# First norm applied at the evictions, x loaded in column blocks, and state space tables built from repeated rows

## What is computed

```python
h = rms_norm(x, norm_g)                      # x * rsqrt(mean(x*x) + eps) * g
g_q, g_k, ..., f_gate = split(h @ w_in)      # first layer: linear attention and forgetting attention
...
bb_re = coef_re[..., None] * br_ - coef_im[..., None] * bi_     # S5 layer: 128 groups of 16 channels,
bb_im = coef_re[..., None] * bi_ + coef_im[..., None] * br_     # 64 complex states each
```

## Time and profile before

| | |
|---|---|
| median of 3 runs | 3414.6 us (3409.22 to 3414.64) |
| profiled execution | 3409.54 us, span 3407.7 us |
| TensorE, VectorE, ScalarE, GpSimd busy | 98%, 48%, 38%, 15% |
| granted TensorE clock, mean | 0.994 |

### The profile page before, as it was taken

One profiled execution on the slowest core, in us unless ns is written; L12 is line 12 of the kernel. 1 busy time (PEld: TensorE's weight loads), 2 busy tenths in 40 slices (PEclk: granted clock), 3 DMA queues, 4 the chain that ended last, 5 costly groups with the idle time before them and its releaser, 6 DMA issues.

```text
span 3407.7 us, 41780 instructions
## 1 busy us (share of the span) xinstructions
PE 3330.7 (98%) x16431; PEld 2695.1 (79%) x16431; DVE 1635.8 (48%) x2695; ACT 1304.6 (38%) x2010; POOL 515.3 (15%) x749
## 2 busy tenths in 40 slices
PE   7999999999999999999999999999999999999998
PEld 6777887888888888888888776788878888777886
DVE  7895654344343444444344655553424343355433
ACT  4443433343233333433242646532323323355432
POOL 0001312322110000110330111121000111110211
PEclk8999999999999999999999999999999999999999
DMA  6776433546348777454335443363433643433642
GB/s 208 221 226 200 135 106 102 159 137 220 131 160 225 200 210 211 153 171 129 128 107 179 128 142 107 124 207 124 142 88 115 205 146 117 133 112 109 205 147 93
DMA packets 279523, 525.06 MB, mean 154 GB/s; under 512 B 64189, under 2 KB 99588, under 8 KB 274720
## 3 DMA queue, kind: packets, MB, share of 16 engines
q1 hardware_dynamic: 223504, 340.79, 33.2%
q0 software_dynamic: 53648, 178.32, 15.4%
q10 hardware_dynamic: 2176, 3.28, 0.4%
HBM read 408.32 MB, written 113.97 MB: 153 GB/s over the span
## 4 chain that ended last, share of the span: by engine, by line
PE 73%; ACT 3%; DVE 3%; issue 2%; DMA 1%; POOL 0%; ACTq 0%; POOLq 0%; DVEq 0%
PE pg L631 64%; PE pm L1322 2%; PE pm L1351 2%; PE pm L1338 1%; PE pm L2423 1%; ACT whi L390 1%; DMA mx_g<-zt 1%; PE pm L2427 0%; PE pm L2411 0%; DVE d_x L2511 0%; ACT stage L501 0%; ACT w_p L1387 0%; PE pm L2402 0%; PE pm L1816 0%; DVE wlo L396 0%
## 5 line engine op out<-in xcount | busy, mean ns | idle before, releaser
L396 DVE TENSOR_TENSOR wlo<-raw,whi 128x1024 fp32r<-128x1024 f32 x523 | 662.3, 1271 | 1237.1 <-ACT whi L390 1236.1
L390 ACT ACTIVATE whi<-raw 128x1024 fp32r<-128x1024 f32 x523 | 548.9, 1054 | 1093.6 <-PE pg L631 1084.0
L631 PE MATMUL pg<-a_hi,whi 128*128 128x512 f32 x1856 | 742.6, 400 | 11.2 <-DVE wlo L396 4.7
L631 PE MATMUL pg<-a_hi,wlo 128*128 128x512 f32 x1856 | 725.8, 391 | 0.0
L631 PE MATMUL pg<-a_lo,whi 128*128 128x512 f32 x1856 | 724.9, 391 | 0.0
L631 PE MATMUL pg<-b_hi,whi 128*128 128x512 f32 x1568 | 622.8, 397 | 7.4 <-DVE stage L572 3.2
L631 PE MATMUL pg<-b_hi,wlo 128*128 128x512 f32 x1568 | 612.2, 390 | 0.0
L631 PE MATMUL pg<-b_lo,whi 128*128 128x512 f32 x1568 | 611.7, 390 | 0.0
L631 PEld LDWEIGHTS pg<-a_hi,whi 128*128 128x128 f32 x1856 | 347.7, 187 | 90.2 <-issue 14.3
L631 PEld LDWEIGHTS pg<-a_hi,wlo 128*128 128x128 f32 x1856 | 347.2, 187 | 77.3
L631 PEld LDWEIGHTS pg<-a_lo,whi 128*128 128x128 f32 x1856 | 348.0, 187 | 73.3 <-issue 2.6
(11 more groups left out here) (442 smaller groups left out, 3846.1 us busy)
## 6 DMA issues: line engine op xcount, KB each, us to landing
raw<-in_l_w_in SPq DMA_DIRECT2D x169, 512.0 KB, 3.7
raw<-in_ab_w_in SPq DMA_DIRECT2D x112, 512.0 KB, 3.8
zt<-stage POOLq DMA_DIRECT2D x142, 256.0 KB, 3.5
raw<-in_c_w_in SPq DMA_DIRECT2D x64, 512.0 KB, 5.3
raw<-in_l_w_out SPq DMA_DIRECT2D x64, 512.0 KB, 4.0
raw<-in_ab_w_out SPq DMA_DIRECT2D x32, 512.0 KB, 4.0
raw<-in_glu_w SPq DMA_DIRECT2D x32, 512.0 KB, 4.1
raw<-in_c_w_out SPq DMA_DIRECT2D x32, 512.0 KB, 3.7
```

What stands on the lines that cost most here:

```text
L390: nc.scalar.activation(used(whi, n), used(raw, n), ACT.Copy).then_inc(hi_ready, 1)
L396: nc.vector.tensor_tensor(used(wlo, n), used(raw, n), used(whi, n).bitcast(F32), ALU.subtract).then_inc(lo_ready, 1)
L631: ins = nc.tensor.matmul(pg[m][:r.rows(m), :r.cols()], lhsT, rhs, start=(kt == 0 and n_pass == 0), stop=(kt == r.kts - 1 and n_pass == 2))
```

## The change

Two parts. **First norm at evictions.** `GLA_IN`, `FOX_IN` and `AB_GATES` join the scaled phases: the operand is x times the gain alone, and the evictions multiply by the deviation (transposed regions by VectorE at L572, the others by ScalarE). x is loaded in column blocks of 2, 2, 5 and 7 tiles; four tiles are turned before the first product and twelve within the first six half pieces after the first. ScalarE squares the token rows at half pieces 7 to 10, into `stage`. SyncE loads pieces 0 to 2 before the state space parameters and all other vectors. The first layer's attention uses a tile of its own instead of `rstd`. The preparation starts behind 7 pieces instead of 4.

**Tables by rows.** The powers are turned once (8 transposes) and stored; for each slice scaled B is turned (2 transposes) and stored as rows, and four loads of 512 KB (`repeat_rows`) bring both back repeated over 128 partitions, where VectorE multiplies them one slice later. `s_L` and its 16 transposes per slice are gone; `s_BT` is stored by its own semaphore.

```diff
-    SCALED = {n: C_U0 for n in (C_U0, C_REST)}
+    SCALED = {n: GLA_IN for n in (GLA_IN, FOX_IN, AB_GATES)}
+    SCALED.update({n: C_U0 for n in (C_U0, C_REST)})
...
+                r.deviation = 1 if SCALED[n] == GLA_IN else JOINTS[SCALED[n]]["devs"] + 1
...
+    X_BLOCKS = ((0, 2), (2, 4), (4, 9), (9, 16))
+    LAST_FRONT_UNIT = 6
+
     def turn_in_pool(pool):
+        for n, (k0, k1) in enumerate(X_BLOCKS):
+            if n == 2:
+                pool.wait_ge(raw_in[2], 16)
+            columns = slice(k0 * P, k1 * P)
+            pool.dma_start(XT["x_tok"][:, :, columns], inp["x"][0, :, columns].rearrange("(t p) d -> p t d", p=P)).then_inc(tokens_moved[n], 16)
+
+    def x_landed(eng, kt):
+
+        for n, (k0, k1) in enumerate(X_BLOCKS):
+            if k0 <= kt < k1:
+                eng.wait_ge(tokens_moved[n], 16)
+
+    def front_tiles(unit):
+
+        return range(2 * unit + 2, 2 * unit + 4) if 0 < unit <= LAST_FRONT_UNIT else ()
...
+        for kt in range(MT):
+            turn_x_pe(pe, kt)
+        pe.wait_ge(cols_ready, 1)
...
+    def first_block_pe(pe, unit):
+
+        for kt in front_tiles(unit):
+            turn_x_pe(pe, kt)
+        if unit == 10:
+            pe.wait_ge(s5_th, 1)
+            pe.wait_ge(xt_ev, 13)
+            for i in range(3):
+                ins = nc.tensor.transpose(pm[0][:, i * NPAIR:(i + 1) * NPAIR], s5_natural(i), ident[:NPAIR, :NPAIR])
+            ins.then_inc(s5_ct, 1)
+        if unit == 12:
+            pe.wait_ge(consts_in, 16 * NCONST)
+            pe.wait_ge(xt_ev, KT)
+            for r in range(2):
+                w = min(NROWS - r * P, P)
+                ins = nc.tensor.transpose(pm[1][:, r * P:r * P + w], rows[:w, r, :], ident[:w, :w])
+            ins.then_inc(cols_turned, 1)
+            pe.wait_ge(sd_ready, 1)
+            for t in range(NTOK):
+                ins = nc.tensor.matmul(pm[2][:, t * P:(t + 1) * P], rstd_col[:, t:t + 1].broadcast_to([P, P]), ident[:, :], start=True, stop=True)
+            ins.then_inc(rs_ready, 1)
...
+        split_hi(act, 0)
+        act.wait_ge(cols_ready, 1)
+        for kt in range(MT):
+            operand_hi(act, kt)
+        split_hi(act, 1)
+        split_hi(act, 2)
...
+    def first_block_act(act, unit):
+
+        for kt in front_tiles(unit):
+            operand_hi(act, kt)
+        if 7 <= unit < 7 + NTOK:
+            t = unit - 7
+            for c in range(NTOK):
+                act.wait_ge(tokens_moved[c], 16)
+            if t:
+                act.wait_ge(acc_done, KT // NTOK * t)
+            nc.scalar.activation(stage[:, :, :].rearrange("p m t -> p (m t)"), XT["x_tok"][:, t, :], ACT.Square,
+                                 accum_out=rstd_col[:, t:t + 1]).then_inc(acc_done, KT // NTOK)
+        if unit == 11:
+            s = lambda n: T5["s_small"][:, n, :]
+            act.wait_ge(acc_done, KT)
+            serial(act, act_seq)(nc.scalar.activation(rstd_col[:, :], rstd_col[:, :], ACT.Ln, scale=1.0 / D, bias=eps[:, 0:1]))
+            nc.scalar.activation(rstd_col[:, :], rstd_col[:, :], ACT.Exp, scale=-0.5).then_inc(sd_ready, 1)
...
+    def operand_lo(dve, kt):
+
+        dve.wait_ge(xt_ev, kt + 1)
+        dve.wait_ge(nh_ready, kt + 1)
+        nc.vector.scalar_tensor_tensor(out=A["a_lo"][:, kt, :], in0=XB["xb"][:, kt, :], scalar=col("ab_norm_g", kt),
+                                       in1=A["a_hi"][:, kt, :].bitcast(F32), op0=ALU.mult, op1=ALU.subtract).then_inc(h_ready, 1)
+
+    def tiles_dve(dve, tiles):
+
+        for n, kt in enumerate(tiles):
+            dve.wait_ge(xt_ready, kt + 1)
+            nc.vector.tensor_copy(XB["xb"][:, kt, :], pm[kt % 4][:, :]).then_inc(xt_ev, 1)
+            if n:
+                operand_lo(dve, kt - 1)
+        for kt in tiles[-1:]:
+            operand_lo(dve, kt)
 
     def turn_in_dve(dve):
+        dve.wait_ge(cols_turned, 1)
+        nc.vector.tensor_copy(cols[:, :KT], pg[3][:, :KT]).then_inc(cols_ready, 1)
+        dve.wait_ge(cols_ready, 1)
+        for kt in range(2):
+            dve.wait_ge(xt_ready, kt + 1)
+            nc.vector.tensor_copy(XB["xb"][:, kt, :], pm[kt][:, :]).then_inc(xt_ev, 1)
+        split_lo(dve, 0)
+        for kt in range(2):
+            operand_lo(dve, kt)
+        tiles_dve(dve, range(2, MT))
+        split_lo(dve, 1)
+        split_lo(dve, 2)
...
+        def repeat_rows(sl):
+
+            js = slice(sl * SPAIR, (sl + 1) * SPAIR)
+            over_rows = lambda name, n: V5[name][:, n, :, :].rearrange("p j x -> p (j x)")
+            for n in range(2):
+                power = powers_rows[n][:, js, :].rearrange("e j x -> e (j x)").unsqueeze(1)
+                sp.dma_start(over_rows("s_Pr", n), power.broadcast_to([ST, SC, SPAIR * P])).then_inc(rows_repeated, 16)
+                b = b_rows[sl][n].rearrange("(a c j) x -> a c (j x)", a=1, c=SC)
+                sp.dma_start(over_rows("s_Br", n), b.broadcast_to([ST, SC, SPAIR * P])).then_inc(rows_repeated, 16)
...
+            if at == 0 and sl == 0:
+                sp.wait_ge(s5_bte, 1)
+                sp.dma_start(powers_rows.rearrange("n (h e) j x -> (e j) (n h) x", e=2), V5["s_BT"][:, 0, :, :]).then_inc(rows_kept, 16)
+            if at == 3 and 0 < sl <= SSL:
+                sp.wait_ge(s5_l, 2 * sl)
+                sp.dma_start(bt_dram[sl - 1], V5["s_BT"][:, :, :, :].rearrange("p n j x -> p (n j x)")).then_inc(b_tables_kept, 16)
+            if at == 3 and 0 <= sl < SSL:
+                sp.wait_ge(s5_bte, sl + 2)
+                sp.dma_start(b_rows[sl].rearrange("n p x -> p n x"), V5["s_bT"][:, :, :]).then_inc(rows_kept, 16)
+            if at == 4 and 0 <= sl < SSL:
+                sp.wait_ge(rows_kept, 16 * (sl + 2))
+                repeat_rows(sl)
             if at == 5 and 0 <= sl < SSL:
-                sp.wait_ge(s5_bte, 2 * sl + 2)
-                keep(bt_dram, V5["s_BT"][:, :, :, :].rearrange("p n j x -> p (n j x)"), sl)
...
-        def turn_b(sl, n):
-            pe.wait_ge(s5_l, 2 * sl + n + 1)
-            if n == 0:
-                pe.wait_ge(s5_cc, sl + 1)
-            else:
-                pe.wait_ge(s5_ke, sl)
-            for j in range(SPAIR):
-                ins = nc.tensor.transpose(pm[2 * n + j // 4][:, j % 4 * P:(j % 4 + 1) * P], V5["s_L"][:, n, j, :, :], ident[:, :])
+        def turn_powers():
...
+        def turn_b(sl):
+            pe.wait_ge(s5_b, sl + 1)
+            pe.wait_ge(s5_bte, sl + 1)
+            for n in range(2):
+                ins = nc.tensor.transpose(pm[3][:, n * P:(n + 1) * P], V5["s_B"][:, n, :, :].rearrange("p c j -> p (c j)"), ident[:, :])
+            ins.then_inc(s5_bt, 1)
...
         def b_powers(sl, n):
-            js = slice(sl * SPAIR, (sl + 1) * SPAIR)
-            power = lambda c: ang[:, c, :ST, js].rearrange("p e j -> p j e").unsqueeze(3).broadcast_to([P, SPAIR, ST, SC])
-            b3 = lambda x: V5["s_B"][:, x, :, :].unsqueeze(2).broadcast_to([P, SPAIR, ST, SC])
             if n == 0:
-                dve.wait_ge(s5_b, sl + 1)
-                dve.wait_ge(s5_sc, 3)
-            else:
+                dve.wait_ge(rows_repeated, 16 * ROW_LOADS * (sl + 1))
+                dve.wait_ge(rows_kept, 16)
+                dve.wait_ge(b_tables_kept, 16 * sl)
+            to, by, tp = V5["s_BT"][:, n, :, :], V5["s_Pr"], t.rearrange("p j e c -> p j (e c)")
+            run(tt(to, V5["s_Br"][:, n, :, :], by[:, 0, :, :], ALU.mult))
+            run(tt(tp, V5["s_Br"][:, 1 - n, :, :], by[:, 1, :, :], ALU.mult))
+            tt(to, to, tp, ALU.subtract if n == 0 else ALU.add).then_inc(s5_l, 1)
+            if n == 0:
                 dve.wait_ge(s5_l, 2 * sl + 1)
...
-                if at in (1, 2):
-                    b_powers(sl, at - 1)
                 if at in (3, 4):
                     c_powers(sl, at - 3)
                 if at == 5:
                     phase(sl)
                 if at == 5 and sl == 0:
                     own_channel()
+            if at in (1, 2) and 0 < sl <= SSL:
+                b_powers(sl - 1, at - 1)
...
+        load_piece(sp, 0)
+        sp.wait_ge(made, 7)
+        vector("ab_norm_g", ident_in)
+        load_piece(sp, 1)
+        load_piece(sp, 2)
+        for n, name in enumerate(("s5_lambda_re", "s5_lambda_im")):
+            sp.dma_start(s5_natural(n), inp[name][0].rearrange("(j g) p -> j (g p)", g=2)).then_inc(s5_nat, 16)
+        sp.dma_start(T5["s_pw"][:NPAIR, 1, 0, :2], inp["s5_log_step"][0].rearrange("(j g) -> j g", g=2)).then_inc(s5_nat, 16)
+        sp.dma_start(T5["s_kv"][:, :], inp["steps"][:, :]).then_inc(s5_nat, 16)
+        load_piece(sp, 3)
...
-        beside(prep_sp(sp), PREP_STEPS, sp, sp_piece, GLA_IN, 4)
+        beside(prep_sp(sp), PREP_STEPS, sp, sp_piece, GLA_IN, 7)
```

238 lines of the change are left out of this document (104 added, 134 removed).

## The result

The changed kernel takes 3512.5 us (median of 4 runs, 3505.7 to 3516.0), the kernel before 3414.6 on the same chip: a ratio of 1.0284, 95% interval [1.0271, 1.0298]. It is 98 us slower; I had forecast 3418, with 3446 as the upper end. The profiled execution has a span of 3511.4 us, against 3407.7.

What follows compares the result with a forecast made beforehand. TensorE, 98% busy, was taken as the bound, VectorE right behind and binding in the new slices. The preparation stage summed to 306.7 against 304.5 us (+2.2), moved evictions +1.4: +3.6, giving 3418; range 3398 to 3446.

Steps and rivals of the forecast that it cites:

- The start: Kernel start: first product at 11.3 us (bounds 10 and 14), first 12 matmuls cold, no stall before 60.
- The lead steps and the slices without waits: State space preparation: lead steps 19.0 us, slices 1 to 7 bound by VectorE at 174.5 us before waits.
- Rows in time: Rival, slices: stored rows and loads land 4 us or more earlier, few waits; -17 us, 3398; chance 0.24.
- The stores: SyncE, each slice: the 1 MB table store lands in 6.6 us, the small rows store hardly earlier.
- Four loads are 2.1 MB, 5.0 us at 419 GB/s, and about 2.5 us of fixed time: Repeated row loads of a slice: land in 7.5 us as plain loads do, 15.2 if one after another.
- I summed 20.9: Slices 1 to 7: VectorE's waits for the repeated rows, 20.9 us in all.
- A piece is needed some 20 us after its issue, so these are covered: SyncE's queue: later pieces behind its wait for the rows store are issued early enough.
- Half rate: Rival, repeated loads: first dimension 8 uses half the engines, 10 instead of 5 us; +31, 3445; chance 0.30.
- two signs: New profile: four loads landing in 12 us or more, DMA share about 0.5 where they run alone, mean half-rate loads.
- the f_nc loads: Evidence against half-rate loads: broadcast loads elsewhere, 256 KB in 4.1 us, aren't slow though they repeat over 128.
- VectorE elsewhere: Rival, linear attention stage: evictions wait for VectorE, seven blocks at 2 us; +14 more, 3430; chance 0.12.
- My +1.4: Behind the first product stage: 28 evictions moved from ScalarE to VectorE cost TensorE 1.4 us.

Runs made afterwards that it cites:

- order_plain: Changed kernel with B and C loads earlier on SyncE, the table store ahead of the row loads, and 128 plain weight rows per load: 3419.6 us.
- front_alone: Kernel before with only the first part (norm at evictions, x in column blocks, later preparation), tables as before: 3414.9 us, ratio 1.0007.
- eight_plain: Changed kernel with each row load reading 128 different weight rows, source pattern (8, 16, 1024), nothing repeated: 3512.0 us.
- first_dim_16_input: Changed kernel with row loads in a (16, 8) pattern with repeats, reading weight rows, table stored in one piece: 3455.7 us.
- before_no_phase: Kernel before with the phase table's five VectorE operations replaced by one clear in slices 1 to 7: 3411.9 us.
- before_tight_steps: Kernel before with only the preparation steps spread otherwise: lead steps in 3 half pieces, slices in 69, last in 2: ratio 1.0000.
- tables_alone: Kernel before with only the tables by rows, on the old start with 4 lead pieces: 3511.5 us, ratio 1.0281.
- front_tight_act: Kernel before with the first part alone, preparation steps spread otherwise, and two of five phase operations per slice on ScalarE: 3403.8 us, ratio 0.9968.
- order_16_store_first: Changed kernel with B and C loads earlier on SyncE, row loads with first dimension 16, table store ahead of them: 3439.2 us.

## Why the prediction was wrong

**The start: right.** First product at 11.71 (forecast 11.3), cold matmuls behind it, one stall of 2.62 us for the third x block, none longer before 60.

**The lead steps and the slices without waits: too short.** I had slice 0 start at 79; VectorE's row has 83.6 in the changed kernel. I had VectorE at 174.5 us for slices 1 to 7, 24.9 each; order_plain, in which rows are hardly waited for, has 27.1. Five and 15 us: this is why the rival *Rows in time* (-17) does not exist either, for the milestone of order_plain is 2.5 us later than before, not 17 earlier. I took VectorE's occupied time from one slice of the kernel before and assumed that it would run through without gaps; even in front_alone, where VectorE is 97% busy at best and 90% from 100 to 300 us, a slice takes 26.2 (first turns of its tables from 91.90 to 275.41 in seven slices).

**The stores: right, and priced too long.** The rows store lands in 4.3 us (median), the table store in 4.2; I had 6.6.

**"Four loads are 2.1 MB, 5.0 us at 419 GB/s, and about 2.5 us of fixed time": the step that failed.** 18.2 and 20.7 us from issue to use, in place of 7.5, and outside the bounds of 7.5 to 15.2. Two things are in it. The loads run on 8 of 16 engines (eight end events a load, share 0.50; eight_plain against first_dim_16_input, 3512.0 against 3455.7: 56 us). And they don't run alone: the C table, a piece and the phase table are issued right behind them and share those engines. I priced the four as one stream at 419 GB/s; they land one after another. Waits for rows of 103.8 us (95.2 in slices 1 to 7, 8.6 behind them) stand where I summed 20.9; that difference of 83 is most of the 94 by which the milestone was missed.

**"A piece is needed some 20 us after its issue, so these are covered": wrong, and it closed the loop.** I held SyncE to be gated in some slices only, and counted what is queued behind its own wait, but not what is queued behind a piece that waits for VectorE: the B and C loads of the next slice, for which TensorE waits 80.2 us. A wait in VectorE delays a split, the split a piece, the piece these loads and the stores, and those the next rows. The order alone is worth 23 us with plain rows (3442.9 to 3419.6), and 19.5 on half the engines, there with the table store behind the loads (3512.5 to 3493.0).

**The rival Half rate: the right mechanism at half its price.** I gave it 0.30 and 3445. It added 27 us to the forecast, 5 us for each landing and 4 at the end, and left SyncE's loop open; measured, the step from 16 to 8 costs 54 to 56 us. Its two signs, a landing of 12 us or more and a DMA share of about 0.5, both came. What I set against it, the f_nc loads, repeat over 128, so they could say nothing about an 8. It was the case that came, and the range should have reached much further above it.

**VectorE elsewhere: not seen.** With 41 more evictions by VectorE than the 83 of the earlier trace rows they hold TensorE for 9.6 us in all instead of 4.2, but some 5.5 us of that stand ahead of the milestone; behind it, with the 28 more, they hold it for 4.2 us in three waits, as before. The times behind the milestone agree: 3088.9 us in the changed kernel (3511.4 - 422.5) and 3091.0 in front_alone, against 3081.5 in the kernel before (3407.7 - 326.2), 3088.4 in before_no_phase (3413.1 - 324.7), 3090.0 in before_tight_steps and 3090.3 in tables_alone, all four with the evictions of before. My +1.4 can't be told from nothing in that scatter, and the rival's +14 is not there.

The sum of part 2, from the runs: half the engines 56 us, pattern (16, 8) against 128 rows 9 to 13, SyncE's order 23, the rest 5; together 93 to 97 of 98. They are the steps of one chain of edits; taken in another order the steps differ (the order is worth 19.5 us on half the engines). The single executions among them are certain to some 5 us each.

## What to carry to other kernels

Before a broadcast load is costed by its bytes, read the first dimension of its source pattern: 8 in front put the loads on half of the engines and cost 54 to 56 us. Turning the pattern to 16 took a few lines, one of them a permuted store that cost some 16 us itself; a version with 128 in front and the right rows was not built. When a step adds a wait to an engine that also frees buffers, follow the circle through the DMA queue to the end: whatever stands in order behind a load that is gated by that engine is late too. And when two engines are both close to full, an earlier start of one wins only what the other can follow; give the other its share first (an earlier first step, work moved to a third engine), then start sooner.

## What I had not expected of the hardware

- Work moved from VectorE to GpSimd came back: 128x1152 operations of 1.36 us took up to 2.47 beside GpSimd's, so that 2.3 us less a slice gave nothing. A part of the same work on ScalarE (1.1 us a slice, front_tight_act) did pay.
- One 4 KB row read 128 times is no slower than 128 rows (3446.7 and 3442.9 us, single executions), whereas a permuted store of 1 MB took 7.1 us instead of 4.2 and delayed what stood behind it.
- SyncE can stand at an issue itself: in order_16_store_first, behind four row loads and four other large transfers issued in the 15 us before, two small loads took 7.59 us to issue, where the pair just ahead took 1.34. What it waits for there is not shown:

```profile
199.63 1.34 SPq L2132 DMA_DIRECT2D s_b<-in_s_b_re  x2
201.01 7.59 SPq L2132 DMA_DIRECT2D s_b<-in_s_b_im  x2
```
